# First norm and projections: a load moved up, an addition moved to VectorE, loads issued earlier, two groups of products exchanged

## The reference

```python
cm = _modulation(c_ctx, w_mod[i], b_mod[i], 2 if last else 6)       # silu(c) @ w + b
hc = _rmsnorm(ctx, norm_mix_pre[i]) * (1.0 + cm[1]) + cm[0]
sf_c = _state_features(hc, w_in[i], ...)
hx = _rmsnorm(x, norm_mix_pre[i]) * (1.0 + sc1) + sh1
rk, rv, gk, gv, log_a, beta = _state_features(hx, w_in[i], ...)     # projections with w_in
rq, rg, gq, gz, gates = _query_features(hx, w_in[i], gdn_conv[i])
```

## Time and profile before

| | us |
|---|---|
| median of three runs | 3336.83 |
| lowest and highest of them | 3332.36, 3341.05 |
| the profiled execution | 3329.19 |
| its span, first to last instruction | 3327.3 |

### The profile page before, as it was taken

One profiled execution on the slowest core, in us unless ns is written; L12 is line 12 of the kernel. 1 busy time (PEld: TensorE's weight loads), 2 busy tenths in 40 slices (PEclk: granted clock), 3 DMA queues, 4 the chain that ended last, 5 costly groups with the idle time before them and its releaser, 6 DMA issues.

```text
span 3327.3 us, 34278 instructions
## 1 busy us (share of the span) xinstructions
PE 2872.6 (86%) x14021; PEld 1437.2 (43%) x14021; DVE 978.4 (29%) x1607; ACT 458.0 (14%) x957; POOL 610.6 (18%) x433
## 2 busy tenths in 40 slices
PE   4998599998998989997999779678688988888887
PEld 2644567775443545443544333344222222222232
DVE  2041645554113351111111258662212111121122
ACT  2011222221101211111111111341000000000000
POOL 1001255642200114342434210311000000000000
PEclk7999799999998999998999989887899999999999
DMA  5010044332322349997999721123799999999997
GB/s 224 27 63 14 23 140 130 118 121 86 114 76 92 143 183 373 384 369 275 370 377 359 275 98 51 41 106 130 282 421 420 420 421 420 421 420 421 421 420 291
DMA packets 127475, 793.24 MB, mean 238 GB/s; under 512 B 21954, under 2 KB 22338, under 8 KB 56920
## 3 DMA queue, kind: packets, MB, share of 16 engines
q1 hardware_dynamic: 102616, 744.32, 55.8%
q0 software_dynamic: 22880, 37.81, 4.7%
q10 hardware_dynamic: 1824, 8.91, 0.7%
HBM read 769.37 MB, written 38.86 MB: 243 GB/s over the span
## 4 chain that ended last, share of the span: by engine, by line
PE 61%; DMA 23%; DVE 9%; issue 3%; ACT 2%; POOL 1%; SPq 0%; POOLq 0%; ACTq 0%; DVEq 0%
DMA arena<-in_w_down 12%; PE b L2853 10%; PE b L1795 6%; DMA yd<-arena 6%; PE b L1359 5%; PE b L474 3%; PE b L476 3%; PE b L1809 3%; PE b L2888 2%; DMA arena<-h2d,arena 2%; PE b L2375 2%; PE b L615 2%; PE b L1047 2%; PE b L1060 2%; PE b L1423 2%
## 5 line engine op out<-in xcount | busy, mean ns | idle before, releaser
L2853 PE MATMUL b<-arena 128*64 128x512 f32 x2048 | 456.5, 601 | 23.2 <-DMA arena<-in_w_up 10.1
L1795 PE MATMUL b<-arena 128*64 128x256 f32 x3072 | 355.1, 383 | 3.0 <-DMA arena<-in_w_gu 1.8
L2868 PE MATMUL b<-arena 128*64 128x512 f32 x1024 | 245.1, 603 | 60.7 <-DMA arena<-in_w_down 60.6
L2853 PEld LDWEIGHTS b<-arena 128*64 128x64 f32 x2048 | 153.7, 137 | 320.3 <-issue 262.8
L1795 PEld LDWEIGHTS b<-arena 128*64 128x64 f32 x3072 | 212.8, 137 | 114.2 <-issue 4.1
L2113 POOL DMA_INDIRECT yd<-arena x96 | 152.5, 1588 | 354.1 <-ACT arena L1896 163.5
L1809 PE MATMUL b<-arena 128*64 128x512 f32 x768 | 186.0, 604 | 1.0 <-issue 0.9
L2068 DVE TENSOR_TENSOR arena<-arena,b 128x128 f32<-128x128 f32 x96 | 27.8, 290 | 515.6 <-ACT arena L1886 478.1
L1359 PE MATMUL b<-arena 128*128 128x512 f32 x384 | 166.8, 596 | 9.6 <-DMA arena<-in_w_in 9.6
L2868 PEld LDWEIGHTS b<-arena 128*64 128x64 f32 x1024 | 64.5, 135 | 240.7 <-DMA arena<-in_w_down 141.0
L2964 DVE TENSOR_TENSOR arena<-arena,b 128x512 f32<-128x512 f32 x32 | 20.6, 686 | 467.7 <-PE b L2853 467.7
(11 more groups left out here) (469 smaller groups left out, 3707.3 us busy)
## 6 DMA issues: line engine op xcount, KB each, us to landing
arena<-in_w_gu SPq DMA_DIRECT2D x65, 2048.0 KB, 10.3
arena<-in_w_gate SPq DMA_DIRECT2D x128, 1024.0 KB, 27.0
arena<-in_w_up SPq DMA_DIRECT2D x128, 1024.0 KB, 26.1
arena<-in_w_down SPq DMA_DIRECT2D x128, 1024.0 KB, 25.3
arena<-in_w_dn SPq DMA_DIRECT2D x65, 1024.0 KB, 13.2
arena<-in_w_mod SPq DMA_DIRECT2D x80, 512.0 KB, 3.8
arena<-in_w_in SPq DMA_DIRECT2D x19, 2048.0 KB, 8.5
arena<-yd SPq DMA_DIRECT2D x12, 512.0 KB, 7.9
```

The costliest lines, as they stand in the source:

```text
L1795: x = e.matmul(ps[i % 2][64 * j:64 * j + 64, 0:256], XGT[i % 2][:, k % 4, (k // 4) * 64:(k // 4) * 64 + 64], GUB[place_of(w)][:, k, j * 25 ...
L2853: x = e.matmul(ps[b + c][64 * hf:64 * hf + 64, :], XS[q % 2][:, kb, (n % 2) * 64:(n % 2) * 64 + 64], w[:, u * 512:(u + 1) * 512], start=(k ...
L2868: x = e.matmul(ps[4][64 * hf:64 * hf + 64, :], H[:, c * 4 + j, hi * 64:hi * 64 + 64], w[:, i * 1024 + hf * 512:i * 1024 + hf * 512 + 512], ...
```

## The change

It has four parts.

1. in_cT_2 becomes SP's second DMA, in place of its last in this stage.
2. Norm has a new form, `shared=False`, for this first norm: DVE adds the shift itself behind its scaling, ACT copies both halves out, and POOL has no part in it. The later norms keep the old form.
3. SP in projections no longer waits for the end of the norm but for the last w_mod product (the counter `first_mm` at "rows"); the buffers that it loads lie where pieces of w_mod were.
4. The six ab groups stand behind the eight g groups, before v. TensorE's wait for w_ab stands at their head.

```diff
-    def __init__(self, K, name, tiles, bufs, trash, ssc, dstT, banks):
+    def __init__(self, K, name, tiles, bufs, trash, ssc, dstT, banks, shared=True):
+        self.shared = shared
...
         e.wait_ge(*self.dve.at(n, "scaled", i))
-        e.tensor_tensor(b, b, self.tiles[i][2], ALU.add).then_inc(*self.pool.up(n, i))
+        e.tensor_tensor(b, b, self.tiles[i][2], ALU.add).then_inc(*(self.pool if self.shared else self.dve).up(n, "row", i))
...
     def out_act(self, e, i):
         n, col = self.name, self.tiles[i][3]
-        e.wait_ge(*self.mm.at(n, i, 0))
-        e.activation(self.dstT[:, 0:4, col:col + 128], heads(self.bank(i, 0)[:, :]), ACT.Copy).then_inc(*self.act.up(n, "out", i))
+        for half in range(1 if self.shared else 2):
+            e.wait_ge(*self.mm.at(n, i, half))
+            e.activation(self.dstT[:, half * 4:half * 4 + 4, col:col + 128], heads(self.bank(i, half)[:, :]),
+                         ACT.Copy).then_inc(*self.act.up(n, *self.last(half), i))
...
             self.scale(e, i)
-            if i:
+            if not self.shared:
+                self.shift(e, i)
+            elif i:
                 self.out_dve(e, i - 1)
-        self.out_dve(e, len(self.tiles) - 1)
+        if self.shared:
+            self.out_dve(e, len(self.tiles) - 1)
...
         e.dma_start(K.scT[0], I["cT"]).then_inc(*came_c.up())
+        e.dma_start(K.scT[1], I["cT_2"]).then_inc(*came_c2.up())
...
-        e.dma_start(K.scT[1], I["cT_2"]).then_inc(*came_c2.up())
...
     def pool(e):
         rows.done(e)
-        norm.shifts(e)
...
-    groups = [("ab", 0, GAB[:, t, :], t, "A" if t % 2 == 0 else "V") for t in range(6)]
+    groups = []
...
+        if ci == 1:
+            groups += [("ab", 0, GAB[:, t, :], t, "A" if t % 2 == 0 else "V") for t in range(6)]
...
-        K.norm1.done(e)
+        e.wait_ge(*K.first_mm.at("rows"))
         e.dma_start(wab, I["w_ab"]).then_inc(*came_ab.up())
...
-        e.wait_ge(*came_ab.at())
         for i, (kind, ci, dst, where, _) in enumerate(groups):
-            if ci and i == of(ci)[0]:
-                e.wait_ge(*came_w[ci % 2].at(ci))
+            if i == of(ci)[0]:
+                e.wait_ge(*(came_w[ci % 2].at(ci) if ci else came_ab.at()))
```

More of the change, by code:

```diff
@@ L226, in shift, with row @@
         e.wait_ge(*self.dve.at(n, "scaled", i))
-        e.tensor_tensor(b, b, self.tiles[i][2], ALU.add).then_inc(*self.pool.up(n, i))
+        e.tensor_tensor(b, b, self.tiles[i][2], ALU.add).then_inc(*(self.pool if self.shared else self.dve).up(n, "row", i))
+    def row(self, e, i):
+        e.wait_ge(*(self.pool if self.shared else self.dve).at(self.name, "row", i))
     def transpose(self, e, i):
         n, nb, N = self.name, len(self.bufs), len(self.banks)
-        e.wait_ge(*self.pool.at(n, i))
+        self.row(e, i)
         for half in range(2):
@@ L234, in transpose @@
             if before >= 0:
-                e.wait_ge(*(self.dve if before % 2 else self.act).at(n, "out", before // 2))
+                e.wait_ge(*(self.dve if self.shared and before % 2 else self.act).at(n, *self.last(before % 2), before // 2))
             for q in range(4):
@@ L238, in transpose, with last @@
             x.then_inc(*self.mm.up(n, i, half))
+    def last(self, half):
+        return ("out",) if self.shared or half else ("first",)
     def out_act(self, e, i):
         n, col = self.name, self.tiles[i][3]
-        e.wait_ge(*self.mm.at(n, i, 0))
-        e.activation(self.dstT[:, 0:4, col:col + 128], heads(self.bank(i, 0)[:, :]), ACT.Copy).then_inc(*self.act.up(n, "out", i))
+        for half in range(1 if self.shared else 2):
+            e.wait_ge(*self.mm.at(n, i, half))
+            e.activation(self.dstT[:, half * 4:half * 4 + 4, col:col + 128], heads(self.bank(i, half)[:, :]),
+                         ACT.Copy).then_inc(*self.act.up(n, *self.last(half), i))
     def out_dve(self, e, i):
@@ L274, in out @@
         e.wait_ge(*self.act.at(self.name, "out", i))
-        e.wait_ge(*self.dve.at(self.name, "out", i))
+        if self.shared:
+            e.wait_ge(*self.dve.at(self.name, "out", i))
     def done(self, e):
@@ L345, in first_rows @@
     norm = Norm(K, "mix1", [(K.X[:, i, :], A1x, S1x, i * 128) if i < 4 else (cx[:, i - 4, :], A1c, S1c, i * 128)
-                            for i in range(6)], hb, ring[1][:, 0:1024], ss, K.HT, range(8))
-    K.norm1 = norm
+                            for i in range(6)], hb, ring[1][:, 0:1024], ss, K.HT, range(8), shared=False)
+    K.norm1, K.first_mm = norm, mm
     def sp(e):
         e.dma_start(K.scT[0], I["cT"]).then_inc(*came_c.up())
+        e.dma_start(K.scT[1], I["cT_2"]).then_inc(*came_c2.up())
         e.dma_start(msb[:, 0, :], I["bmod"][:, 0, :]).then_inc(*came_b.up("first"))
@@ L1342, in sp @@
                 e.dma_start(wr[2], I["w_in_2"][4]).then_inc(*came_w[2].up("v"))
-            e.wait_ge(*norm.pool.at("ffn1", t))
+            e.wait_ge(*norm.pool.at("ffn1", "row", t))
             e.dma_start(K.h2d[t * 128:(t + 1) * 128, :], norm.bufs[t]).then_inc(*kept.up(t))
@@ L2766, in sp @@
                 for t in range(4):
-                    e.wait_ge(*norm.pool.at("ffn2", t))
+                    e.wait_ge(*norm.pool.at("ffn2", "row", t))
                     e.dma_start(K.h2d[t * 128:(t + 1) * 128, :], H2[:, t, :]).then_inc(*kept.up(t))
@@ L3003, in pool @@
         norm.shifts(e)
-        e.wait_ge(*norm.pool.at("ffn2", 3))
+        e.wait_ge(*norm.pool.at("ffn2", "row", 3))
         for o in range(2):
```

## The result

| five executions each | before | after |
|---|---|---|
| median, us | 3336.83 | 3321.36 |
| lowest and highest, us | 3332.36, 3341.05 | 3318.47, 3323.69 |
| the profiled execution, us | 3329.19 | 3318.47 |
| its span, us | 3327.3 | 3316.7 |

The ratio of after to before is 0.9955, with an interval of 0.9944 to 0.9966: 15.0 us faster by the ratio, where 12.1 were forecast. Timed again on another occasion it was 3316.63 (3310.21 to 3326.07), with a ratio of 0.9956 (0.9940 to 0.9972).

What follows compares the result with a forecast made beforehand. TensorE was taken as the bound from 72.00 us on, for 243 us, so an earlier first projection shifts everything behind it. Gains 2.2 + 6.2 + 1.9 + 1.8 = 12.1 us, 3336.8 to 3324.7; range 3316 to 3331.5.

Steps and rivals of the forecast that it cites:

- By-heads: Stage that follows the projections; its first product was to come 12 us earlier, the terms' sum being 12.1.
- start of the norm: Condition vector in_cT_2 second in SP's queue: ACT's first square at 40.0 instead of 42.2, gain 2.2 us.
- norm by VectorE: First norm, six tiles: DVE sets a period of 2.68 us, 18.8 us instead of 25.0, gain 6.2.
- wait for w_ab gone: Between norm and projections: issue and flight of w_ab, 70.05 to 72.00, disappear; gain 1.9 us.
- clock: Projections, g first and ab second: ab holds the high clock 4.1 us, less slower climbs; net gain 1.8 us.
- 9 turns, each against a w_mod packet of 8 KB: in_cT_2's load on SP's queue: costs 2.5 us, 1.1 back, net 1.4; consts land at 34.7 instead of 33.3.
- the first Rows product: After consts at 34.7: ready for ACT 2.1 us after its start at the low clock, first take at 36.8.
- the second rival: SP's queue: the vector costs nothing, consts at 33.3, x sets the start at 38.7; 1.3 us more, 3323.4; chance 0.10.
- The first rival: Projections: ab keeps the high clock, taking 10.3 us, and v has no climb; 20.2 us gained, 3316.6; chance 0.08.
- Given back later: Stages behind 320 us: clock and indirect-load waits may meet the shifted start otherwise; no change, 3336.8; chance 0.11.
- Slower, w_in in front of x: Loads before the norm: w_in packets delay x to 56.7, norm start 16.7 us later than forecast, 3341.4; chance 0.04.

Runs made afterwards that it cites:

- part 1 alone: Kernel before with only in_cT_2 moved to second on SP's queue; one execution 3338.13 us, beside 3330.41 of before; by-heads 2.0 us earlier than before.
- ab 64 wide: Changed kernel with each ab product 64 columns wide, the same 16 columns read four times; one execution, by-heads 19.8 us earlier than before.
- four small loads: Changed kernel with four more loads of in_cT_2, into unused tiles, right behind the first on SP's queue; by-heads 11.2 us earlier than before.
- POOL's additions for nobody: Changed kernel with GpSimd adding a tile of its own to itself seven times during the norm; g began 10.4 us later, by-heads 4.1 earlier than before.
- part 2 alone: Kernel before with only the first norm's new form (VectorE adds shifts, ScalarE copies both halves); by-heads 5.6 us earlier than before.
- shared norm: Changed kernel with GpSimd adding the first norm's shifts again and VectorE copying second halves; by-heads 7.9 us earlier than before.
- the spread groups: Changed kernel with one ab group behind each of the first six pairs of wide groups; median 3312.81 us, ratio to before 0.9937 (0.9918 to 0.9956).
- The second profile: Changed kernel, unchanged, profiled on a second occasion; median 3316.63 us, ratio to before 0.9956; by-heads 14.1 and end 18.9 us earlier than before.

## Why the prediction was right, and where it was not

The median came out 3.3 us below the forecast of 3324.7, inside the range and on the side forecast as likeliest. By-heads moved by 14.1 where 12.1 were forecast: 1.5 of the 2.0 between lie in the start, 0.4 in the clock. The steps, in the order of the sum:

| term | forecast | measured |
|---|---|---|
| start of the norm | 2.2 | 42.18 - 38.49 = 3.7 |
| norm by VectorE | 25.0 to 18.8, 6.2 | 60.06 - 41.37 = 18.7, 6.3 |
| wait for w_ab gone | 1.9 | 1.9 (72.00 - 70.05 against 0.05) |
| clock | 1.8 | 14.1 - 11.9 = 2.2 |
| by-heads | 12.1 | 14.1 |

**Start of the norm: mis-sized by 1.5 us.** Two steps were off. The first, 1.1 us, is "9 turns, each against a w_mod packet of 8 KB": consts landed at 33.64, 0.4 later than before, where 1.4 were reckoned to 34.7. That a packet takes its turn whatever its size is borne out for the four further loads, 283 to 283; but this one load passed in its first half us at 104 to 34. The Trainium skill, "DMA: Bandwidth & Descriptors", section "Queues, rings and completion order", has an engine pass a whole packet of some 9 to 17 descriptors before it turns to the other queue; that would fit this first half us, and not the even counts in the stretches of half a us behind it. The second step, 0.4 us, is the first Rows product: 2.1 us to ACT's first take, at the low clock, where after had 1.6, since the granted clock was still 1.00 until about 34.3. Where it was 0.50 from the first of these products on (part 1 alone, ab 64 wide), consts to square took 5.4 us, near the 5.3 forecast; in after it took 4.85.

What set the start was not x, as the second rival had it. x landed at 3.76 + 34.4 = 38.2, before the square, and the square came 0.5 us behind ACT's last take of a Rows product in every profile, also where x had landed at 27.9 (four small loads). The rival was right about the queue, rated too low at 0.10; its start of 38.7 is near the measured 38.49 by luck.

**The norm: right by its steps.** The period was 2.66 for 2.68, scaling and addition 1.29 and 1.23 as taken, the end 18.7 for 18.8. The reason given, that DVE is at its own pace once POOL is silent, was argued from two rows and is now shown: POOL's additions for nobody alone make it 5.66, and the loads beside it change nothing (part 2 alone, shared norm).

**The early loads: right in the sum, wrong as a price of the part.** 1.9 us is what disappears between the kernels before and after. But the prediction did not say that moving g to the front needs the loads early: without them g waits 9.7 us. Undoing the parts one at a time gives 3.6, 6.1, 9.8 and 3.1, together 22.6, and not 14.1.

**The clock: right direction, two of three sizes just outside their bounds.** ab kept 1.00 for 5.3 us (bounds 3.3 to 5.0), g climbed for 4.9 (2.9 to 4.5), v for 3.6, inside. ab took 15.35 us for some 16.5. In the sum: 5.3 saved, less the 3.1 by which g and v together took longer (43.96 + 70.70 against 111.54), is the 2.2 of by-heads; half of the climbs makes 2.8 of the 3.1. The 2.2 is small by luck of the pair, since before had the shortest climb of all; over the groups of profiles above, the order is worth about 3.1. That ab would not hold the clock was right. That it takes narrow products in a row for the fall is shown by the spread groups, which held 1.00 in both profiles that have them; that the width counts rests on one profile with 64 columns. The first rival's 64-column rows were good evidence for 64 columns alone, as the prediction had it.

**Given back later.** The profiled pair looks like it: 14.1 us at by-heads, 10.6 at the end. The second profile has the same 14.1 and ends at 18.9, so there is spread, as the prediction put it, and no loss that these runs show. One piece of it is the router's clock, 4 us either way; the rest wasn't located. In the medians the gain of 15.0 us is the 14.1 of by-heads, to within the interval.

**Slower, w_in in front of x.** It didn't occur: x landed 0.5 us earlier than before, and w_in waited its turn behind consts and ctx.

## What to carry to other kernels

Where VectorE and GpSimd alternate on the same tiles, count the slowdown of both engines beside each other before giving GpSimd a share: here one engine alone took 18.7 us for six tiles, and the pair 25.0. Don't put products of few columns in a long row; strewn among wide ones group by group, or made wider with useless columns, they took 10.1 and 10.7 us here, and in a row 15.0 to 15.8 behind wide ones and 20.6 ahead of them. And price a part of a change at the place where its neighbours leave it, by undoing it as well as by doing it alone; read that at the end of its stage, not at the end of the program.

## What the runs showed of the hardware

- TensorE at 100% busy with products of 16 columns never came from a granted clock of 0.50 to 1.00 in 20.6 us, and fell from 1.00 after 4.8 to 5.7 us in seven profiles. 64 columns kept 1.00 through 10.66 us behind g, but the router's, of the same width, kept it in seven profiles and lost it in seven, once each way with the same kernel (7.3 and 11.4 us). Whether 64 columns are safe is thus open.
- The climb to 1.00 with g's wide products took 2.7 (before) to 5.9 us (ab 64 wide), which moves a stage by 1.6 us with no change in its work.
- VectorE's scaling went from 1.29 to 2.73 us and its addition from 1.23 to 2.80 beside GpSimd's additions on other data, and GpSimd's own took 2.63 where they had taken 2.35. DMA at full flow (423 to 442 GB/s from 38 to 46 us) beside the norm's first tiles changed neither.
- Packets of 64 bytes and of 4 to 8 KB stood one to one where both queues had work (106 to 107, 283 to 283), but for the first half us of SP's loads (104 to 34). A load of 128 rows of 64 bytes in front of large loads delayed its queue by 0.4 us against before, and each of four more by 1.0.
